# First FFN matrix: plain form for the first pair of feature tiles only, seven-product form from the second pair on, with the feature sums in another order

## The reference, cut to what matters

```
h = rmsnorm(x, norm_pre_ffn) * (1.0 + sc_f) + sh_f      # 512 x 1024
gate, up = split(h @ w_ffn_in, 2)                       # 512 x 2816 each
y = (silu(gate) * up) @ w_ffn_out
```

## Time and profile before

| | us |
|---|---|
| median of 3 runs (lowest, highest) | 680.82 (680.43, 680.99) |
| the profiled execution | 681.38 |
| its span | 679.6 |
| PE busy | 664.2 (98%) |
| DVE busy | 592.4 (87%) |
| ACT busy | 378.4 (56%) |
| POOL busy | 159.2 (23%) |

### The profile page before, as it was taken

One profiled execution on the slowest core, in us unless ns is written; L12 is line 12 of the kernel. 1 busy time (PEld: TensorE's weight loads), 2 busy tenths in 40 slices (PEclk: granted clock), 3 DMA queues, 4 the chain that ended last, 5 costly groups with the idle time before them and its releaser, 6 DMA issues.

```text
span 679.6 us, 12900 instructions
## 1 busy us (share of the span) xinstructions
PE 664.2 (98%) x4580; PEld 555.2 (82%) x4580; DVE 592.4 (87%) x976; ACT 378.4 (56%) x647; POOL 159.2 (23%) x129
## 2 busy tenths in 40 slices
PE   7999999999999999999999999999999999999996
PEld 6566678777777878888788999999999998887785
DVE  4787989898898998988997699999999989859986
ACT  7367664646564443544773355555556557646554
POOL 4000000000000000000004376676676643410200
PEclk9999999999999999999999999999999999999999
DMA  8973222232213665669244344444543538996903
GB/s 276 358 215 100 63 64 63 63 124 62 63 44 112 202 181 201 222 202 287 70 133 116 94 118 132 126 126 119 154 125 91 154 125 131 216 262 196 186 2 123
DMA packets 104350, 96.82 MB, mean 142 GB/s; under 512 B 2975, under 2 KB 87027, under 8 KB 104310
## 3 DMA queue, kind: packets, MB, share of 16 engines
q1 hardware_dynamic: 98870, 85.82, 41.4%
q0 software_dynamic: 5440, 10.49, 9.0%
HBM read 94.20 MB, written 2.10 MB: 142 GB/s over the span
## 4 chain that ended last, share of the span: by engine, by line
PE 55%; DMA 4%; DVE 3%; issue 2%; POOL 1%; ACT 0%; DVEq 0%; POOLq 0%
PE ps L2419 26%; PE ps L1889 9%; PE ps L2467 8%; DMA w_raw<-in_w_ffn_out 4%; PE ps L1908 3%; PE ps L1926 3%; PE ps L2253 1%; PE ps L2233 1%; POOL w_raw L601 1%; PE ps L2390 1%; DVE w_lo L1710 1%; PE ps L2397 1%; PE ps L1947 1%; PE ps L2392 1%; PE ps L2246 0%
## 5 line engine op out<-in xcount | busy, mean ns | idle before, releaser
L1889 PE MATMUL ps<-h_hl,w_hi 128*128 128x512 f32 x544 | 174.4, 402 | 1.2 <-DVE w_lo L1143 1.2
L1889 PEld LDWEIGHTS ps<-h_hl,w_hi 128*128 128x128 f32 x544 | 98.4, 188 | 26.5 <-issue 5.5
L1889 PE MATMUL ps<-h_hl,w_lo 128*128 128x512 f32 x272 | 106.3, 391 | 0.0
L2419 PE MATMUL ps<-h_hl,w_hi 128*128 128x256 f32 x576 | 104.5, 283 | 0.0
L2467 PE MATMUL ps<-w_hi,ht_hl 128*128 128x512 f32 x312 | 97.5, 391 | 1.6 <-DVE ht_hl L1716 1.5
L2419 PEld LDWEIGHTS ps<-h_hl,w_hi 128*128 128x128 f32 x576 | 90.0, 192 | 0.2
L2419 PE MATMUL ps<-h_hl,w_lo 128*128 128x256 f32 x288 | 81.5, 283 | 0.0
L2419 PE MATMUL ps<-ht_hl,w_hi 128*128 128x256 f32 x432 | 78.5, 283 | 0.0
L2467 PEld LDWEIGHTS ps<-w_hi,ht_hl 128*128 128x128 f32 x312 | 58.5, 188 | 15.7 <-DVE w_lo L1710 2.3
L2419 PEld LDWEIGHTS ps<-ht_hl,w_hi 128*128 128x128 f32 x432 | 67.4, 192 | 0.0
L1143 DVE TENSOR_TENSOR w_lo<-w_raw,w_hi 128x1024 fp32r<-128x1024 f32 (+1 forms) x50 | 58.6, 1178 | 4.9 <-ACT w_hi L611 4.3
(11 more groups left out here) (336 smaller groups left out, 1351.7 us busy)
## 6 DMA issues: line engine op xcount, KB each, us to landing
w_raw<-in_w_ffn_in SPq DMA_DIRECT2D x44, 512.0 KB, 4.5
w_raw<-in_w_in SPq DMA_DIRECT2D x28, 512.0 KB, 4.0
w_raw<-in_w_ffn_out POOLq DMA_DIRECT2D x14, 512.0 KB, 7.4
act<-in_w_ada SPq DMA_DIRECT2D x12, 512.0 KB, 8.5
adaw<-in_w_ada SPq DMA_DIRECT2D x6, 1024.0 KB, 5.2
act<-in_w_ada SPq DMA_DIRECT2D x6, 1024.0 KB, 5.2
res<-in_x SPq DMA_DIRECT2D x8, 512.0 KB, 5.6
w_raw<-in_w_out SPq DMA_DIRECT2D x8, 512.0 KB, 5.3
```

Source lines behind the costliest of these rows:

```text
L1889: last = mm(ps[bank][0:rows, :], a, b, start=(k == 0 and n == 0), stop=(k == KT - 1 and n == 2))
L2419: last_mm = mm(ps[bank][:, 0:HALF], a, b, start=(start and k == 0 and n == 0), stop=(k == 3 and n == 2), skip_group_check=not start)
```

## The change: what it does

FIRST_PAIR goes from 2 to 1, so that pair 1 is computed in the seven-product form as pairs 2 to 10 are. TensorE loses the four plain groups of pair 1 and runs one more pair of `win_tile`. ACT and DVE lose the four splits and the two silus and multiplications of plain pair 1, and have the feature sums in a written order between the steps of the first seven-product tile. `add_tail(1)` moves into the first `win_pair`. SP loads pair 1 at the same points as before; pair 2 is loaded by the loop.

```diff
-PAIRS, FIRST_PAIR = FT // 2, 2
+PAIRS, FIRST_PAIR = FT // 2, 1
@@ SyncE
             load_tail(1)
-            for v in range(2):
-                for half in range(2):
-                    sp.wait_ge(lo_ok, G_WIN - 3 + 2 * v + half)
-                    load_fin(FIRST_PAIR, v, half)
-            load_tail(2)
             with sp.Fori(FIRST_PAIR + 1, KT + 1) as i:
@@ ScalarE
             plain_silu(0, 0)
-            split_hi(0, U_FIN[0] + 1, G_FIN + 1)
-            split_hi(1, U_FIN[1] + 1, G_FIN + 2)
             feature_sum_hi(0)
+            win_hi(FIRST_PAIR, 0, 0)
+            feature_sum_hi(1)
+            win_hi(FIRST_PAIR, 0, 1)
+            feature_sum_hi(2)
+            win_hi(FIRST_PAIR, 0, 2)
             plain_silu(0, 1)
-            split_hi(2, U_FIN[2] + 1, G_FIN + 3)
-            split_hi(3, U_FIN[3] + 1, G_FIN + 4)
-            feature_sum_hi(1)
-            feature_sum_hi(2)
-            plain_silu(1, 0)
-            win_hi(FIRST_PAIR, 0, 0)
-            win_hi(FIRST_PAIR, 0, 1)
-            plain_silu(1, 1)
-            win_hi(FIRST_PAIR, 0, 2)
             win_hi(FIRST_PAIR, 0, 3)
             feature_sum_hi(3)
@@ VectorE
             plain_swiglu(0, 0)
-            split_lo(G_FIN + 4, 0)
-            split_lo(G_FIN + 5, 1)
             feature_sum(1)
+            win_lo(FIRST_PAIR, 0, 0)
             feature_sum(2)
             feature_sum_lo(0)
+            feature_sum_lo(1)
+            win_lo(FIRST_PAIR, 0, 1)
+            feature_sum(3)
+            feature_sum_lo(2)
+            win_lo(FIRST_PAIR, 0, 2)
             plain_swiglu(0, 1)
-            split_lo(G_FIN + 6, 2)
-            split_lo(G_FIN + 7, 3)
-            feature_sum(3)
-            feature_sum_lo(1)
-            feature_sum_lo(2)
-            plain_swiglu(1, 0)
-            win_lo(FIRST_PAIR, 0, 0)
-            ve.wait_ge(gate_bias, 32)
-            add_tail(1)
-            win_lo(FIRST_PAIR, 0, 1)
-            plain_swiglu(1, 1)
-            win_lo(FIRST_PAIR, 0, 2)
             win_lo(FIRST_PAIR, 0, 3)
             feature_sum_lo(3)
+            ve.wait_ge(gate_bias, 32)
             win_pair(FIRST_PAIR, add_tail)
@@ TensorE
                 for u in range(2, 4):
                     feature_group(G_FIN + u, u, u)
-                for u in range(4):
-                    te.wait_ge(act_ok[u // 2], 1)
-                    feature_group(G_FIN + 4 + u, u, u)
```

## The result

The changed kernel takes 684.37 us (median of 6 runs, 683.96 to 685.52), the kernel before beside it 680.94 (6 runs, 680.43 to 681.12). The ratio is 1.0052 (95% interval 1.0042 to 1.0062): slower by 3.4 us, where the prediction had 1.7 and a range that ended at 683.7. The profiled execution took 684.13 us with a span of 682.3, which is 2.7 over that of before.

What follows compares the result with a forecast made beforehand. The prediction took TensorE, busy for 98% of the span, as the bound. Saving 1.60 us and adding a 3.29 us delay gave +1.7 on 680.82, so 682.5 us, range 679.6 to 683.7.

Steps and rivals of the forecast that it cites:

- TensorE saves 1.60: Pair 1 on TensorE: 21.76 us in plain form becomes 20.16 in seven-product form, saving 1.60 us on the path.
- Pair 1's sums start at about 347.6 and hold DVE: GpSimd's pair 1 weight sums start at about 347.6; the first costs DVE 0.53 us, each later one 1.09.
- The delay up to the first split of the next pair: DVE's split u = 0 of the next pair comes at 384.42, wanted by TensorE at 381.13: delay 3.29 us, the largest.
- the walk: Operation-by-operation count of DVE and GpSimd alternating whole instructions from about 347.6; sums hold DVE 7.26 us up to low 3.
- inside the 1.25: First seven-product tile: ACT's 1.0 us lateness after feature sum 3 is covered by TensorE's 1.25 us wait at u = 2.
- After it DVE gains about 0.6 us on TensorE in each pair ... so nothing is added.: Later pairs: DVE recovers about 0.6 us per pair, from its one idle time of 0.62, adding no further delay.
- a gap at each later pair: Listed sign that the forecast is wrong: TensorE showing a gap at every later pair; no size given.
- the mechanism of the forecast: Around the change of form, GpSimd holds DVE at every turn; net +1.2 to +2.4 us, time 682.5, chance 0.50.
- more held: Rival: every sum holds DVE 1.09, or group 3 waits too; net +3.2 us, time 684.0, chance 0.12.
- The rule on which the forecast leaned: Two-input VectorE instructions in SBUF and GpSimd instructions reading SBUF exclude each other for a whole instruction; 2.31 for 1.22 us.
- shared bandwidth: Alternative for GpSimd's sums beside DVE: both run at 1.22 / 2.1, u = 2 at about 367.3, delay some 0.6 less.

Runs made afterwards that it cites:

- silent sums: Changed kernel with GpSimd's eight weight sums of pair 1 replaced by memsets that read nothing; 679.95 us, ratio to before 0.9982.
- ACT order: Changed kernel with three changes of order on ACT: two first snaps made earlier, the gate-sum copy later; 683.60 us, ratio to before 1.0042.
- Half the tail: Changed kernel with each add_tail addition covering 512 of its 1024 columns; 682.70 us, ratio to before 1.0027.
- before, half tail: Kernel before the change, with each add_tail addition covering 512 of its 1024 columns; 681.25 us, ratio to before 1.0006.

## Why the prediction was wrong: its steps one by one

- **TensorE saves 1.60.** Right: 1.61 with the sums silent. (The prediction also sets this beside a table of the Trainium skill, TensorE: Matmul & The Clock Gate, Back-to-back issue gap, and says that the trace disagrees for the short matmuls. It disagrees for both: 0.227 us against an estimate of 0.216 for 512 columns, 0.120 against 0.109 for 256. The section gives that table for a matmul by itself, not for a stream with a weight load before each, which this kernel has.)
- **Pair 1's sums start at about 347.6 and hold DVE.** Right: 346.82, which with the head start of 0.86 is 347.68, and 2.30 for held operations. The first weight load came at its time too.
- **The delay up to the first split of the next pair.** Size right, way partly other, so the size is in part luck. 1.08 + 1.37 + 0.31 + 0.38 = 3.14 us up to 386.4, forecast 3.29. But the walk assumed strict turns; in the profiled run GpSimd was starved for 4.49 us, so u = 2 came undisturbed at 365.0, low part 3 was done at 368.94 (369.80 with the head start added, walk 372.07), and the delay went through GpSimd, ACT and the snap instead. Where turns were taken ("ACT order"), the walk's intermediate delays held to 0.2. Feature sum 3 at ACT, "inside the 1.25", showed as the stop itself for that reason.
- **"After it DVE gains about 0.6 us on TensorE in each pair ... so nothing is added."** This is the step of the prediction that failed: the term behind the first pair was put at nothing, and measured 1.29 us. The 0.62 of the earlier trace rows is idle time, and I took it for slack. But the split that follows the idle time took 1.23, and now that DVE comes to it without idling, it meets GpSimd's sum and takes 2.02 (DVE's timeline in the changed kernel):

```profile
394.18 2.02 DVE L1695 TENSOR_TENSOR w_lo<-mix,w_hi 128x1024 fp32r<-128x1024 f32 x1
```

  0.62 of idle time are replaced by 0.79 of holding. From the split before it to the addition behind it the old kernel takes 5.67 us (408.59 to 414.26) and the changed one 5.65 (390.47 to 396.12): nothing is gained. DVE therefore stays some 2 us late for 150 us, in which small things that once had cover cost: 0.18 at 406.7, 0.12 in the slips from 427 to 508 and 0.99 at 528 for ACT's gate copy, together 1.29. Half the tail gives 1.33 back, in the changed kernel alone. The prediction had named "a gap at each later pair" among the signs of being wrong, and that sign came.
- **The second matrix.** Not in the prediction, +0.7 (115.0 against 114.3; the profile of every changed kernel has 114.8 to 115.2, of the two old ones 114.3 and 114.6). It is not DVE's lateness: with silent sums it is there too. GpSimd issues the same loads at the same distance from the matrix's start (18.97 and 18.98 for the load into `tail_place`), but ACT's copy that waits for this load starts 28.19 behind the matrix's start before and 28.95 after, and the split behind it and the later ones follow about 0.7 later. ACT before, then after:

```profile
593.49 1.06 ACT L1093 ACTIVATE w_hi<-tail_place 128x1024 fp32r<-128x1024 f32 x1 [1.52 <-DMA tail_place<-in_w_ffn_out]
```

```profile
596.21 1.06 ACT L1082 ACTIVATE w_hi<-tail_place 128x1024 fp32r<-128x1024 f32 x1 [2.61 <-DMA tail_place<-in_w_ffn_out]
```

  Over all the profiles the second matrix is as long as this start is late: 28.19 and 114.3 (before), 28.48 and 114.6 (before, half tail), 28.78 to 29.20 and 114.8 to 115.2 (the changed kernels). The experiment on the old kernel was to tell whether the 0.7 belongs to the change; 114.6 lies between its two answers. What makes the load land later is open; so is whether the head start of 0.86 is a part of the same difference.

The account of the spans: -1.60 + 3.14 + 1.29 = 2.83, + 0.7 in the second matrix, - 0.86 of head start, = 2.7. The medians differ by 3.4: the profiled execution of before took 0.44 more than its median (681.38, 680.94), that of after 0.24 less (684.13, 684.37). In which stretch this 0.7 lies isn't shown, since the times of single stretches are only to be had from a profile. So of the 1.7 us by which the forecast was exceeded, 1.1 are in the first matrix (2.83 against 1.69) and have a shown cause; the rest has none. By the prediction's rivals: the mechanism of the forecast decided, and "more held" came close in price (684.0) but not in mechanism: the sums held DVE for no longer than the walk had it.

The rule on which the forecast leaned (the Trainium skill, SBUF — State Buffer, Who interferes with whom) was the right one against shared bandwidth: held operations take 2.30 and not some value between. That each gets its turn after one instruction is the prediction's own reading of the rows, and it didn't hold here: GpSimd stood through three of DVE's (4.49 us for an operation of 1.30).

## What to carry to other kernels

An idle time of an engine that another can hold (here DVE by GpSimd) need not be slack: compare its pace per loop turn with the bounding engine's (here 20.18 to 20.20 against 20.16) and ask what the next instruction would meet if it came earlier. Where that pace is no smaller, a delay put in at the start of the loop stays to its end, and each instruction on a third engine that had cover from it has to be priced with the delay added. And before shortening the bounding engine's work, ask what the replaced form gave the helpers: here 21.76 us of plain matmuls that need no weight sums, in which DVE was busy for 14.49 us and GpSimd (with pair 2's sums) for 10.45, so that DVE got ahead.

## What the runs showed of the hardware that was not expected

- GpSimd reading SBUF and DVE with two operands in SBUF don't always take turns. The same pair of streams gave turns (GpSimd 2.20, DVE 2.31) in three profiles and a starved GpSimd (4.49 for an operation of 1.30, DVE at its undisturbed 1.14 step) in three others.
- A DMA load issued at the same offset from the second matrix's start (18.97 and 18.98) let the copy that waits for it start at 28.19 in the old kernel and at 28.95 in the changed one, 0.76 us apart.
